# Input in smaller first transfers, a later weight, a later norm total and a last unit in halves

## The reference, cut to what matters

```python
def rms_norm(x, g):
    y = x * lax.rsqrt(jnp.mean(x * x, axis=-1, keepdims=True) + EPS)
    return y * g
def swiglu(h, w_gate, w_up, w_down):
    return (jax.nn.silu(h @ w_gate) * (h @ w_up)) @ w_down
def first_block(x, ...):
    x = x + 0.5 * swiglu(rms_norm(x, ffn1_norm), ffn1_w_gate, ffn1_w_up, ffn1_w_down)
    ...
def second_block(x, ...):
    ...
    merged = g_hy * u_hy + g_at * u_attn
    return x + merged @ w_out
```

## Time and profile before

| | us |
|---|---|
| median of 3 runs (1698.3 to 1698.88) | 1698.82 |
| the profiled execution | 1698.62 |
| its span, first to last instruction | 1696.5 |
| PE busy | 1683.4 (99%) |
| POOL, DVE, ACT busy | 716.1, 1031.8, 642.0 |

### The profile page before, as it was taken

One profiled execution on the slowest core, in us unless ns is written; L12 is line 12 of the kernel. 1 busy time (PEld: TensorE's weight loads), 2 busy tenths in 40 slices (PEclk: granted clock), 3 DMA queues, 4 the chain that ended last, 5 costly groups with the idle time before them and its releaser, 6 DMA issues.

```text
span 1696.5 us, 21151 instructions
## 1 busy us (share of the span) xinstructions
PE 1683.4 (99%) x7666; PEld 1375.3 (81%) x7666; DVE 1031.8 (61%) x1220; ACT 642.0 (38%) x899; POOL 716.1 (42%) x303
## 2 busy tenths in 40 slices
PE   9999999999999999999999999999999999999999
PEld 7887888887788888888888888888777668888887
DVE  6767576527665456458665557786564753969451
ACT  5222222235665656321322322213545754343221
POOL 3444344444343431344444444444355433444443
PEclk9999999999999999999999999999999999999999
DMA  5332233325211221242433232332252023233243
GB/s 195 101 109 92 76 100 99 115 72 194 87 63 63 90 73 38 75 136 91 136 99 110 89 98 90 112 101 89 94 186 75 26 88 130 93 100 99 91 144 113
DMA packets 42815, 171.04 MB, mean 101 GB/s; under 512 B 4937, under 2 KB 5065, under 8 KB 41452
## 3 DMA queue, kind: packets, MB, share of 16 engines
q1 hardware_dynamic: 38736, 148.13, 26.9%
q10 hardware_dynamic: 3996, 21.73, 3.6%
HBM read 159.22 MB, written 10.62 MB: 100 GB/s over the span
## 4 chain that ended last, share of the span: by engine, by line
PE 68%; issue 21%; POOL 6%; DVE 2%; ACT 1%; DMA 0%; POOLq 0%; SPq 0%; DVEq 0%; ACTq 0%
PE psum L306 20%; PE psum L308 20%; PE psum L307 20%; POOL wlo L272 6%; PE psum L1200 1%; PE psum L1213 1%; PE psum L1744 1%; PE psum L1721 1%; PE psum L751 1%; PE psum L736 0%; DMA raw<-wk_dram 0%; PE psum L722 0%; PE psum L1190 0%; DVE psum L444 0%; PE psum L1693 0%
## 5 line engine op out<-in xcount | busy, mean ns | idle before, releaser
L272 POOL TENSOR_TENSOR wlo<-raw,whi 128x1024 fp32r<-128x1024 f32 (+2 forms) x258 | 663.8, 2573 | 893.2 <-ACT whi L294 892.7
L294 ACT ACTIVATE whi<-raw 128x1024 fp32r<-128x1024 f32 (+2 forms) x259 | 286.1, 1105 | 706.6 <-PE psum L308 696.5
L306 PE MATMUL psum<-h_hi,whi 128*128 128x512 f32 x1360 | 537.1, 395 | 2.7 <-POOL wlo L272 1.8
L308 PE MATMUL psum<-h_hi,wlo 128*128 128x512 f32 x1360 | 529.7, 389 | 0.0
L307 PE MATMUL psum<-h_lo,whi 128*128 128x512 f32 x1360 | 529.6, 389 | 0.0
L306 PEld LDWEIGHTS psum<-h_hi,whi 128*128 128x128 f32 x1360 | 255.4, 188 | 63.6 <-POOL wlo L272 4.7
L307 PEld LDWEIGHTS psum<-h_lo,whi 128*128 128x128 f32 x1360 | 255.4, 188 | 53.5 <-issue 2.2
L308 PEld LDWEIGHTS psum<-h_hi,wlo 128*128 128x128 f32 x1360 | 255.3, 188 | 53.5
L306 PE MATMUL psum<-mid_hi,whi 128*128 128x512 f32 x352 | 137.2, 390 | 0.0
L308 PE MATMUL psum<-mid_hi,wlo 128*128 128x512 f32 x352 | 137.0, 389 | 0.0
L307 PE MATMUL psum<-mid_lo,whi 128*128 128x512 f32 x352 | 136.9, 389 | 0.0
(11 more groups left out here) (387 smaller groups left out, 2395.8 us busy)
## 6 DMA issues: line engine op xcount, KB each, us to landing
raw<-wk_dram SPq DMA_DIRECT2D x220, 512.0 KB, 3.5
raw<-wd_dram SPq DMA_DIRECT2D x32, 704.0 KB, 4.1
raw<-wp_dram SPq DMA_DIRECT2D x8, 640.0 KB, 3.8
x_scratch<-xT ACTq DMA_DIRECT2D x2, 2048.0 KB, 8.9
spectra_scratch<-spec_out ACTq DMA_DIRECT2D x4, 1024.0 KB, 5.9
xT<-x_scratch ACTq DMA_DIRECT2D x8, 512.0 KB, 4.5
spec<-spectra_scratch ACTq DMA_DIRECT2D x2, 2048.0 KB, 10.2
xT<-x_dram SPq DMA_DIRECT2D x4, 512.0 KB, 7.6
```

What stands on the lines that cost most here:

```text
L272: pool.tensor_tensor(wlo[s][:, 0:w], raw[s][:, 0:w], whi[s][:, 0:w].bitcast(F32), ALU.subtract).then_inc(lo_ready, 1)
L294: act.activation(whi[s][:, 0:w], raw[s][:, 0:w], ACT.Copy).then_inc(hi_ready, 1)
L306: pe.matmul(dst, s_hi, m_hi, start=start and i == 0, stop=False, **kw)
L308: last = pe.matmul(dst, s_lo, m_hi, start=False, stop=stop and i == n - 1, **kw)
```

## The change

- SP's opening: `xT` in transfers of one, one, two and four chunks, unit 1 behind the third of them, that is, behind four chunks.
- `vec`: the first norm's eight columns in a transfer of their own, the other 123 in a second one that counts on the constants' semaphore; every wait on that semaphore is raised by 16, and ACT and DVE wait for it once in the opening.
- PE's opening: chunks 0, 1, 2 for unit 0, the same for unit 1, then one chunk at a time for both. ACT and DVE prepare unit 1 after chunk 2 instead of chunk 1.
- The first norm's total moves from behind unit 2 to behind unit 3; ACT rounds unit 5 ahead of the factor. The second feed-forward keeps its order.
- The last unit of the program is done as two halves of 256 tokens, in banks 1 and 7, each with its own update; the last four stores are chunks 4 and 5, chunk 6, and the halves of chunk 7.

The diff, cut:

```diff
@@ -346,6 +346,7 @@
         x_landed = [sem(f"x_landed{i}") for i in range(4)]
+        CHUNKS = ((0, 1), (1, 1), (2, 2), (4, 4))
         x_stored = sem("x_stored")
         vec_landed = sem("vec_landed")
         const_landed = sem("const_landed")
@@ -402,7 +403,7 @@
             def tensor(self, pe):
                 if self.i == 0:
-                    pe.wait_ge(const_landed, 16)
+                    pe.wait_ge(const_landed, 32)
                 pe.wait_ge(summed, self.total)
                 pe.matmul(bank(7), ones, sumsq[:, :], start=True, stop=True).then_inc(self.mean, 1)
@@ -509,14 +510,8 @@
             def tensor_first_tiles(self, pe):
                 self.tensor_idle(pe)
-                for k in (0, 2, *range(4, DT), DT):
-                    if k in (0, 2):
-                        turns = ((0, k), (0, k + 1), (1, k), (1, k + 1))
-                    elif k < DT:
-                        turns = ((0, k), (1, k))
-                    else:
-                        turns = ()
-                    for g, c in turns:
+                for chunks in ((0, 1, 2), (3,), (4,), (5,), (6,), (7,)):
+                    for g, c in [(g, c) for g in range(2) for c in chunks]:
                         if c == 0:
                             pe.wait_ge(lo_ready, g + 1)
                         if g == 0:
@@ -543,12 +538,14 @@
                             pe.wait_ge(x_updated, self.x_base)
                         linear(pe, bank(apart), up + 2 * f, h_hi, h_lo, DT, chunk_ready=self.norm.ready if first else None,
                                ready_base=self.norm.base)
-                        if half == 0 and f == 1:
+                        if half == 0 and f == 1 and self.order:
                             self.norm.tensor(pe)
                         pe.wait_ge(lo_ready, up + 2 * f + 2)
                         if half or f > 2:
                             pe.wait_ge(self.mid, freed)
                         linear(pe, bank(1 + apart), up + 2 * f + 1, h_hi, h_lo, DT)
+                        if half == 0 and f == 1 and not self.order:
+                            self.norm.tensor(pe)
                     if half == 0 and self.order == 0:
                         self.tensor_first_tiles(pe)
@@ -586,7 +583,7 @@
                         act.activation(sig[:, :], gate32[:, :], ACT.Sigmoid).then_inc(self.sig, 1)
                     if half == 0:
-                        split_hi_to(act, up + 5)
+                        split_hi_to(act, up + (5 if self.order else 6))
                         self.norm.factor(act)
                         act.preload_act_table(ACT.Sigmoid)
                         sigmoid(0)
...
@@ -1354,10 +1351,15 @@
                         pe.wait_ge(self.gate, self.gates + 2 * DT - 2)
                     else:
                         pe.wait_ge(x_updated, self.x_base + b - 1)
-                    if b:
+                    if b == 0:
+                        self.tensor_first_out(pe)
+                    elif b < DT - 1:
                         linear(pe, bank(b % 2), self.out_base + b, merged_hi, merged_lo, DT)
                     else:
-                        self.tensor_first_out(pe)
+                        self.tensor_last_out(pe)
+
+            def tensor_last_out(self, pe):
+                linear(pe, bank(1), self.out_base + DT - 1, merged_hi, merged_lo, DT)
             def tensor_first_out(self, pe):
                 for c, (hi, lo) in enumerate(weight_chunks(self.out_base, 0, DT)):
@@ -1417,7 +1419,10 @@
                     clear_sum(dve)
                 for b in range(DT):
                     dve.wait_ge(x_landed[b // 2], self.landed)
-                    update_x(dve, self.out_base + b, b, 0, b % 2, 1.0, squares, next_gain)
+                    if squares or b < DT - 1:
+                        update_x(dve, self.out_base + b, b, 0, b % 2, 1.0, squares, next_gain)
+                    else:
+                        self.vector_last_out(dve)
         class FirstMerge(SplitMerge):
...
@@ -2812,6 +2817,24 @@
                     pe.wait_ge(hyena_in.silu, 4)
                     pe.wait_ge(long1.out, 8)
+            def tensor_last_out(self, pe):
+                for g in range(2):
+                    cols = slice(g * T // 2, (g + 1) * T // 2)
+                    last = products(pe, bank(1 + 6 * g)[:, cols],
+                                    [(a, b, merged_hi[:, c, cols], merged_lo[:, c, cols])
+                                     for c, (a, b) in enumerate(weight_chunks(self.out_base + DT - 1, 0, DT))])
+                    last.then_inc(unit_done if g else self.half, 1)
+
+            def vector_last_out(self, dve):
+                for g in range(2):
+                    cols = slice(g * T // 2, (g + 1) * T // 2)
+                    x = xT[:, DT - 1, cols]
+                    if g:
+                        dve.wait_ge(unit_done, self.out_base + DT)
+                    else:
+                        dve.wait_ge(self.half, self.halves + 5)
+                    dve.tensor_tensor(x, x, bank(1 + 6 * g)[:, cols], ALU.add).then_inc(x_updated, 1)
+
             def vector(self, dve):
                 self.vector_merge(dve)
                 self.vector_update(dve, False, None)
@@ -2824,16 +2847,22 @@
         @block.sync
         def _(sp):
             load_unit(sp, 0, 0, "k", 0)
-            for i in range(4):
-                sp.dma_start(xT[:, 2 * i:2 * i + 2, :], x_in[:, 2 * i:2 * i + 2, :]).then_inc(x_landed[i], 16)
-                if i == 0:
+            for i, (k, n) in enumerate(CHUNKS):
+                sp.dma_start(xT[:, k:k + n, :], x_in[:, k:k + n, :]).then_inc(x_landed[i], 16)
+                if i == 2:
                     load_unit(sp, 1, 0, "k", 1)
             sp.dma_start(constf[:, :, :], constf_in).then_inc(const_landed, 16)
             stream_loads(sp)
-            for i in range(4):
+            for i in range(3):
                 sp.wait_ge(x_updated, XS["out2"] + 2 * i + 2)
                 sp.dma_start(out[:, 2 * i:2 * i + 2, :], xT[:, 2 * i:2 * i + 2, :]).then_inc(stored, 16)
-            sp.wait_ge(stored, 64)
+            sp.wait_ge(x_updated, XS["out2"] + DT - 1)
+            sp.dma_start(out[:, DT - 2, :], xT[:, DT - 2, :]).then_inc(stored, 16)
+            for g in range(2):
+                cols = slice(g * T // 2, (g + 1) * T // 2)
+                sp.wait_ge(x_updated, XS["out2"] + DT + g)
+                sp.dma_start(out[:, DT - 1, cols], xT[:, DT - 1, cols]).then_inc(stored, 16)
+            sp.wait_ge(stored, 96)
         @block.gpsimd
         def _(pool):
@@ -2846,16 +2875,18 @@
         @block.scalar
         def _(act):
-            act.dma_start(vec[:, 0:NVEC], vec_in).then_inc(vec_landed, 16)
+            act.dma_start(vec[:, 0:DT], vec_in[:, 0:DT]).then_inc(vec_landed, 16)
+            act.dma_start(vec[:, DT:NVEC], vec_in[:, DT:NVEC]).then_inc(const_landed, 16)
             act.wait_ge(landed[0], 16)
             act.activation(first_hi[:, :], raw[0][:, 0:D], ACT.Copy).then_inc(hi_ready, 1)
             next_hi[0] = 1
             act.wait_ge(vec_landed, 16)
             for k in range(DT):
-                act.wait_ge(x_landed[k // 2], 16)
+                act.wait_ge(x_landed[(0, 1, 2, 2, 3, 3, 3, 3)[k]], 16)
                 act.activation(h_hi[:, k, :], xT[:, k, :], ACT.Copy, scale=col("ffn1_norm", k)).then_inc(gained_hi, 1)
-                if k == 1:
+                if k == 2:
                     split_hi_to(act, 2)
+            act.wait_ge(const_landed, 32)
             split_hi_to(act, 3)
             for k in range(DT):
                 act.activation(first_square[:, k, :], xT[:, k, :], ACT.Square).then_inc(squared, 1)
@@ -2901,10 +2932,11 @@
                 dve.wait_ge(gained_hi, k + 1)
                 dve.scalar_tensor_tensor(h_lo[:, k, :], xT[:, k, :], col("ffn1_norm", k), h_hi[:, k, :].bitcast(F32),
                                          ALU.mult, ALU.subtract).then_inc(gained, 1)
-                if k == 1:
+                if k == 2:
                     dve.wait_ge(hi_ready, 2)
                     dve.tensor_tensor(wlo[1][:, 0:D], raw[1][:, 0:D], whi[1][:, 0:D].bitcast(F32),
                                       ALU.subtract).then_inc(lo_ready, 1)
+            dve.wait_ge(const_landed, 32)
             for k in range(DT):
                 dve.wait_ge(squared, k + 1)
                 dve.wait_ge(summed, k + 1)
```

More of the change, by code:

```diff
@@ L686, in vector_squares @@
                     if b == 0:
-                        dve.wait_ge(const_landed, 16)
+                        dve.wait_ge(const_landed, 32)
                     if b < 4:
@@ L953, in scalar @@
             def scalar(self, act):
-                act.wait_ge(const_landed, 32)
+                act.wait_ge(const_landed, 48)
                 act.activation(constr[:, :, :], constr32[:, :, :], ACT.Copy).then_inc(constr_ready, 1)
@@ L1531, in scalar_inputs @@
             def scalar_inputs(self, act):
-                act.wait_ge(const_landed, 48)
```

(1 more changed line is left out.)

## The result

The changed kernel takes 1702.7 us (median), the kernel before 1698.77 beside it: ratio 1.0023, 95% interval 1.0015 to 1.003, so 3.9 us or 0.23% slower. That lies inside the predicted range; the median is just beyond the bound of 0.2%, and the interval takes that bound in. Three executions took far longer (2410.21 us of the kernel before, 2100.39 of the changed kernel, 5435.9 of the second series of `fold`) and are left out of the ratios. The profiled execution of the changed kernel has a span of 1700.6 us, 4.1 more than before.

What follows compares the result with a forecast made beforehand. PE, busy 1683.4 of 1696.5 us, was taken to bound the kernel. Opening +0.9, the total's move +3.3 and the end -0.95 gave +3.2 on 1698.82: 1702.0 us, range 1699.2 to 1704.4.

Steps and rivals of the forecast that it cites:

- Part 2, the chain behind the total: Total moved behind unit 3: PE waits 2.5 us at unit 6 and 0.75 at unit 7, together +3.3 us.
- S: Start of ACT's split released by the unit before the norm's total, 25.88 us before; the chain's steps count from it.
- the stretched cast: Cast before the second gate, lengthened by a POOL subtraction to 2.37 us; without one taken as 0.43.
- The second wait: PE's further wait, at unit 7, whose low part is ready at S + 20.39 against PE's S + 19.64: 0.75 us.
- The 3.5 us at half speed: Assumed length of PE's low clock after the new wait: 1.75 us lost, 0.75 of it filling unit 7's wait.
- the clock case: Rival, chance 0.22: PE loses its clock in the new wait near unit 6, net +1.0 us, 1703.0, up to 1704.7.
- Part 1, the opening: Second weight behind four tiles lands at least 1.25 us later, three more matmuls meanwhile: +0.9 us (0.55 to 1.25).
- The term for 2 KB rows: In the opening, single-tile transfers with 2 KB rows flow slower, at 279 instead of 438 GB/s: 0.3 us (0 to 0.7).
- The rule that was weighed there: Opening transfers: 512 B suffices for line rate, so 2 KB rows lose nothing and the opening costs 0.57 us.
- the wait for DVE's `wlo`: Sign in the opening: PE waits 1.5 to 2 us near 11 us for the second unit's low part.
- Part 3, the end: Last unit and store in halves: matmuls +0.32, update ends 0.1 earlier, store -0.85; together -0.95 us (-0.6 to -1.05).
- The remark that the move wins nothing: With PE later in the opening, moving the total behind unit 3 gains nothing; with PE earlier, DVE's sums would delay it.

Runs made afterwards that it cites:

- fold: Kernel before with the last unit in halves, unit 1 prepared in two halves, total behind unit 3 and ACT's order from `early_split`: 1697.26 us, second series 1697.46.
- norm_only: Kernel before with only the first norm's total behind unit 3 and unit 5 rounded ahead of the factor: 1702.83 us, ratio 1.0024.
- early_split: Changed kernel with ACT rounding units 6 and 7 ahead of the second and third sigmoid: 1698.76 us, ratio 1.0002 to the kernel before.
- warm: Changed kernel with five matmuls on zeros ahead of PE's wait at unit 6: 1701.82 us.
- experiment 2: The run `norm_back`, 1698.45 us, set beside the kernel before with only the end changed, 1697.79 us.
- norm_back: Changed kernel with the first norm's total back behind unit 2 and unit 5's rounding back behind the first sigmoid: 1698.45 us.
- end_half: Kernel before with the last unit and its store in halves, and unit 1 rounded and subtracted in two halves of four chunks: 1697.87 us.
- weight_second: As `norm_back`, with the second weight loaded behind the first two single chunks and prepared and used there as before: 1698.32 us.

## Why the prediction was right

**Part 2, the chain behind the total.** Every step came where the rows put it: first gate S + 3.76 (reckoned 3.76), second S + 9.13 (9.14), split of unit 6 S + 10.39 (10.40), its low part S + 14.14 (14.20), wait 2.51 (2.5), and unit 7's low part S + 20.33 (20.39). The step that carried it was to take the stretched cast out of the tile (2.37 before, 0.43 after): without that the wait would have come out 1.9 too long. `norm_only` shows that the move does it alone, `early_split` that the rounding behind the second sigmoid is the cause. The second wait is real too: in `warm` unit 7's end lies 4.09 later than before (58.23 against 54.14), 0.73 of it from the opening (unit 2's end, 26.61 against 25.88), so 3.36 for the move at full clock, against 3.3 reckoned.

**The clock was a rival with 0.22 and it happened.** In the profiled execution and in `norm_only` it fell. Its size was 0.8 to 0.9 net (`warm` against the changed kernel), against 1.0 reckoned: seven matmuls at 0.43 instead of 0.227 lose 1.4, and the wait at unit 7 that this covers gives back the 0.6 that it costs in `warm`. The 3.5 us at half speed were near the 3.4 measured (46.1 to 49.5), but by luck: they were chosen between 1 and 5.2 us from slow matmuls at the start, beside which the earlier trace rows show a granted clock of 1.00. So the likeliest time of 1702.0 was that of a kernel whose clock holds, as `warm` shows with 1701.82, and the measured 1702.7 lies between it and the 1703.0 of the clock case; the range held because it had been drawn wide enough for both. The single executions show the two cases side by side: four of twelve have a mean granted clock of 1.000 and took 1701.57 to 1702.01, as in `warm`; the eight at 0.999 took 1701.97 to 1703.50, median 1702.8. So the chance of 0.22 was too low. The end of the trace before, where the clock fell some 2 us after the last matmul, pointed to it, but it was no sure sign (last section).

**Part 1, the opening.** It cost 0.81 in the profiled execution and 0.66 by experiment 2, against 0.9 reckoned. In that execution the place of the weight explains it: PE takes the weight up 1.47 later, 2.38 after its landing as before, and has three more matmuls to do meanwhile, 0.68, which leaves 0.79. The term for 2 KB rows (0.3) is not borne out as chosen: behind four chunks the weight landed at 9.60, 9.28, 9.56 and 9.67 in the changed kernel, `norm_back`, `warm` and `early_split`, against 9.38, 9.51 and 9.34 for the second pair of chunks in three runs with the old order. The means are 0.12 apart, less than the landings scatter. The row that the term was taken from was also misread: the constants were issued at 3.85 and landed 8.8 later, at 12.65, so most of the stretch from 12.5 to 13.0 with 279 GB/s lies behind them. The rule that was weighed there (the Trainium skill, "DMA: Bandwidth & Descriptors", Specifications) was nearer to these 0.12 than that rate, which gave 0.68. One sign missed: the wait for DVE's `wlo` is 1.1, not 1.5 to 2. Part of that idle time stands earlier, because h_lo of the third chunk came late (PE's gap at 9.89), which had been put at nothing; it costs nothing, since PE would wait for `wlo` anyway.

**Part 3, the end.** -0.95 reckoned, -0.91 measured alone. From the last update to the end of the span it is 0.84 less, against 0.85 reckoned for the store. The store's data pass between 1699.2 and 1699.8 (131 GB/s on average in each of the two half microseconds shown), somewhat slower than the 0.31 us reckoned from the rate of the old store.

**The remark that the move wins nothing** was right for this opening and wrong in general: with PE earlier (`end_half`) the sums do hold the total, and the move pays once ACT's order is put right (`fold`).

## What to carry to other kernels

When a result is moved later, follow every in-order queue behind it, not only the engines that use it: here the factor had slack, but two weight roundings stood behind the sigmoids that waited for it, and PE starved. Measure an operation's clean duration from a row where nothing competes, for a shift in time also changes who competes. And count a new wait on TensorE twice, once for its length and once for the clock it may cost; where the wait can't be removed, matmuls on zeros in it are worth a try.

## What the runs showed that I had not expected

The clock's fall need not lie in the wait itself. In `norm_only` PE took up unit 6 at 45.46 and the granted clock was still 1.00 in 45.5 to 46.0; it fell when PE had been at work again for half a microsecond, and held at the lower level until about 49.5.

```profile
45.50:46.00 0.50, 0.50 (x2) 0.45 (x3) 0.47 (x2) 0.00 (x0) 0.00 (x0) 1.00 0.00 0
46.00:47.00 1.00, 1.00 (x4) 0.78 (x3) 0.97 (x2) 0.00 (x0) 0.00 (x0) 0.52 0.66 111
...
49.00:49.50 0.50, 0.50 (x3) 0.41 (x2) 0.40 (x2) 0.00 (x0) 0.50 (x1) 0.54 0.00 0
```

The Trainium skill, "TensorE: Matmul & The Clock Gate" (Part 1: The HAM clock gate), says that activity releases the half clock and idleness brings it back. These rows agree with it; they add that a wait of 2.5 us between two stretches of dense work can be enough. It is not enough each time. At the end of `norm_only` PE is idle from 1696.80 to 1700.6, 3.8 us, and the granted clock stays at 1.00:

```profile
1696.41 0.39 PE L308 MATMUL psum<-merged_hi,wlo 128*128 128x512 f32 x1
```

```profile
1699.00:1700.00 1.00, 0.00 (x0) 0.00 (x0) 0.00 (x0) 0.00 (x0) 0.00 (x0) 1.00 0.73 295
1700.00:1700.60 0.60, 0.00 (x0) 0.00 (x0) 0.00 (x0) 0.00 (x0) 0.00 (x0) 1.00 0.00 0
```

What decides between the two outcomes is not shown by these runs.

A transfer of four chunks releases all four at its end: ACT had the fifth chunk at 12.1 instead of some 1.4 us earlier (10.7 before, when it took `h_hi` of six chunks without a gap from 9.38), and in `weight_second` that delay is where the new transfers' cost shows.
